# The scores' 32x32 diagonal blocks as a step of their own, ahead of each pair's scores

## The reference, cut to what matters

```python
def step(S, inp):                      # _rwkv7_scan, 8 heads of 64
    r_t, w_t, k_t, v_t, kk_t, a_t = inp
    sa = -jnp.einsum('bhvk,bhk->bhv', S, kk_t)
    S = (S * w_t[:, :, None, :] + sa[..., None] * (kk_t * a_t)[:, :, None, :]
         + v_t[..., None] * k_t[:, :, None, :])
    return S, jnp.einsum('bhvk,bhk->bhv', S, r_t)
...
y = lax.conv_general_dilated(z, conv_w, ...)          # causal, depthwise, width 31
return jax.nn.silu(_layernorm(y + conv_b, ln_g, ln_b, LN_EPS))
...
m = jnp.concatenate([o_c, o_d], axis=-1)              # RWKV group, convolution group
x = x + m @ odd_w_out[j]
```

## Time and profile before

| | us |
|---|---|
| median of 2 runs | 1249.18 (1248.44 to 1249.92) |
| the profiled execution | 1249.62 |
| its span, first to last instruction | 1247.8 |
| TensorE busy in the span | 1208.0 (97%) |
| VectorE busy | 640.9 (51%) |
| ScalarE busy | 399.5 (32%) |
| GpSimd busy | 501.3 (40%) |

### The profile page before, as it was taken

The page is one execution under the profiler, slowest core; times in us unless marked ns, Lnnn a source line. Parts: engine busy times, 40 slices in busy tenths (PEclk is TensorE's granted clock), DMA queues, the critical chain, the costliest instruction groups (busy, mean ns, idle before and its releaser), DMA issues. The chain is left out here.

```text
span 1247.8 us, 19837 instructions
## 1 busy us (share of the span) xinstructions
PE 1208.0 (97%) x7876; PEld 968.2 (78%) x7876; DVE 640.9 (51%) x1032; ACT 399.5 (32%) x578; POOL 501.3 (40%) x368
## 2 busy tenths in 40 slices
PE   7999999999999999999999998989999999999996
PEld 6877778888888888887777766757888888888885
DVE  4524655442114544446789889876545211444333
ACT  5634423222112222226353634343322211222110
POOL 0541435554445555545121220113545444555441
PEclk9999999999999999999999999879999999999998
DMA  7211222222322222231111110102222222222211
GB/s 278 102 68 68 74 96 68 101 101 102 101 101 82 89 98 101 101 101 68 35 69 35 36 68 2 35 2 74 96 102 101 101 101 83 86 101 101 101 67 68
DMA packets 17776, 104.97 MB, mean 84 GB/s; under 512 B 1968, under 2 KB 2480, under 8 KB 6064
## 3 DMA queue, kind: packets, MB, share of 16 engines
q1 hardware_dynamic: 17280, 103.67, 23.9%
q10 hardware_dynamic: 432, 0.38, 0.1%
HBM read 101.94 MB, written 2.10 MB: 83 GB/s over the span
## 5 line engine op out<-in xcount | busy, mean ns | idle before, releaser
L580 POOL TENSOR_TENSOR w_lo<-w_raw,w_hi 128x512 fp32r<-128x512 f32 x360 | 495.6, 1406 | 714.4 <-ACT w_hi L673 266.6
L1013 PE MATMUL ps<-h_hi,w_hi 128*128 128x512 f32 x688 | 275.9, 401 | 0.1
L1013 PE MATMUL ps<-h_lo,w_hi 128*128 128x512 f32 x688 | 268.4, 390 | 0.0
L1013 PE MATMUL ps<-h_hi,w_lo 128*128 128x512 f32 x688 | 268.3, 390 | 0.0
L673 ACT ACTIVATE w_hi<-w_raw 128x2048 fp32r<-128x2048 f32 x50 | 95.7, 1913 | 194.7 <-PE ps L1013 143.4
L1013 PEld LDWEIGHTS ps<-h_hi,w_hi 128*128 128x128 f32 x688 | 129.3, 188 | 35.5 <-issue 8.7
L1013 PEld LDWEIGHTS ps<-h_hi,w_lo 128*128 128x128 f32 x688 | 129.4, 188 | 27.6
L1013 PEld LDWEIGHTS ps<-h_lo,w_hi 128*128 128x128 f32 x688 | 129.5, 188 | 25.7 <-issue 1.0
L1013 PE MATMUL ps<-f_hi,w_hi 128*128 128x512 f32 x384 | 149.4, 389 | 0.0
L1013 PE MATMUL ps<-f_lo,w_hi 128*128 128x512 f32 x384 | 149.4, 389 | 0.0
L1013 PE MATMUL ps<-f_hi,w_lo 128*128 128x512 f32 x384 | 149.4, 389 | 0.0
(11 more groups left out here) (328 smaller groups left out, 1699.8 us busy)
## 6 DMA issues: line engine op xcount, KB each, us to landing
w_raw<-in_weights SPq DMA_DIRECT2D x91, 1024.0 KB, 4.8
x<-in_xT SPq DMA_DIRECT2D x8, 256.0 KB, 6.5
w_raw<-in_weights SPq DMA_DIRECT2D x8, 256.0 KB, 6.9
outT<-x SPq DMA_DIRECT2D x8, 256.0 KB, 2.0
sgu_ln<-in_sgu_ln SPq DMA_DIRECT2D x1, 512.0 KB, 7.4
low_w<-in_low_w SPq DMA_DIRECT2D x1, 512.0 KB, 7.1
masks_f<-in_masks SPq DMA_DIRECT2D x1, 432.5 KB, 5.6
sgu_w<-in_sgu_w SPq DMA_DIRECT2D x1, 256.0 KB, 6.4
```

The costliest lines, as they stand in the source:

```text
L580: piece = pool.tensor_tensor(w_lo[:, j, at], w_raw[:, j, at], w_hi[:, j, at].bitcast(f32), SUB)
L1013: mm = pe.matmul(bank(gb(g) if isinstance(i, int) else g % 2), w, r, start=(k == 0 and m == 0), stop=(k == K - 1 and m == 2))
```

## The change

- `scores(c, 4)` becomes a step of its own, `corner(c)`, on TensorE and VectorE. It comes first of a pair's scores: on TensorE it takes the place that `scores(c, 0)` had, on VectorE it stands just before `scores(c, 0)`.
- Its blocks go to banks 4 and 6 instead of 3 and 4. As the scores use bank 6, `scores(c, 0)` now waits for the four corner copies (`x_step`), and the corner waits for `bonus`.
- `scores(c, 0)` moves back on TensorE: in pair 0 to right before scores 1, in pair 1 to one slice before scores 1, in pair 2 to behind `y(1, 3)`, in pair 3 to behind `y(2, 3)`.
- `tok_tr(c, 0)` waits for U of the pair before, where it waited for its Sp.
- The lists around the convolution's norm change too. On TensorE `conv_mean` 0 stands right behind `scores(3, 3)`, `conv_mean` 1 and 2 come among the transposes `tok_tr(3, ·)`, ahead of the last slices; `conv_mean` 3, `conv_var` and `conv_spread` come ahead of `y(3, 2)`, `g(3, 3)`, `u(3, 3)` and `y(3, 3)`. On VectorE `conv_sub`, `conv_root` and `conv_scale` come ahead of `s(3, 2)`. On ScalarE the squares, the root and all four `conv_silu` come ahead of `cut` 58 part 2, `m(2)` and the copies of `g(3, 3)` and `u(3, 3)`.

The diff, cut: first TensorE's list, then the ends of VectorE's and of ScalarE's list (VectorE's list also gets `corner(c)` before `scores(c, 0)` in each pair), then the code of TensorE's and VectorE's steps.

```diff
-            ("slice", 5, 3), ("slice", 5, 4), ("scores", 0, 0), ("slice", 5, 5), ("slice", 5, 6), ("scores", 0, 1),
-            ("slice", 5, 7), ("slice", 7, 0), ("scores", 0, 2), ("slice", 7, 1), ("slice", 7, 2), ("scores", 0, 3),
-            ("scores", 0, 4), *run("slice", 7, 3, 7), ("zw", 1), ("slice", 7, 7), ("tok_tr", 0, 0),
+            ("slice", 5, 3), ("slice", 5, 4), ("corner", 0), ("slice", 5, 5), ("slice", 5, 6), ("scores", 0, 0),
+            ("scores", 0, 1), ("slice", 5, 7), ("slice", 7, 0), ("scores", 0, 2), ("slice", 7, 1), ("slice", 7, 2),
+            ("scores", 0, 3), *run("slice", 7, 3, 7), ("zw", 1), ("slice", 7, 7), ("tok_tr", 0, 0),
...
-            ("slice", 17, 3), ("g", 0, 2), ("scores", 1, 0), ("u", 0, 2), ("slice", 17, 4), ("slice", 17, 5),
+            ("slice", 17, 3), ("g", 0, 2), ("corner", 1), ("u", 0, 2), ("slice", 17, 4), ("slice", 17, 5),
...
-            ("y", 0, 3), *run("slice", 8, 1, 5), ("scores", 1, 1), ("slice", 8, 5), ("slice", 8, 6),
-            ("scores", 1, 2), ("slice", 8, 7), ("slice", 10, 0), ("slice", 10, 1), ("scores", 1, 3),
-            ("scores", 1, 4), *run("slice", 10, 2, 8), ("zw", 2), ("tok_tr", 1, 0), *run("slice", 9, 0, 8),
+            ("y", 0, 3), *run("slice", 8, 1, 4), ("scores", 1, 0), ("slice", 8, 4), ("scores", 1, 1),
+            ("slice", 8, 5), ("slice", 8, 6), ("scores", 1, 2), ("slice", 8, 7), ("slice", 10, 0), ("slice", 10, 1),
+            ("scores", 1, 3), *run("slice", 10, 2, 8), ("zw", 2), ("tok_tr", 1, 0), *run("slice", 9, 0, 8),
...
-            ("y", 1, 1), ("g", 1, 2), ("u", 1, 2), ("slice", 11, 7), ("scores", 2, 0), ("s", 1, 2), ("y", 1, 2),
-            ("g", 1, 3), ("u", 1, 3), ("y", 1, 3), ("slice", 13, 0), ("slice", 13, 1), ("scores", 2, 1),
-            ("slice", 13, 2), ("slice", 13, 3), ("scores", 2, 2), *run("slice", 13, 4, 7), ("scores", 2, 3),
-            ("scores", 2, 4), ("slice", 13, 7), *run("slice", 12, 0, 3), ("tok_tr", 2, 0), ("tok_tr", 2, 1),
+            ("y", 1, 1), ("g", 1, 2), ("u", 1, 2), ("slice", 11, 7), ("corner", 2), ("s", 1, 2), ("y", 1, 2),
+            ("g", 1, 3), ("u", 1, 3), ("y", 1, 3), ("scores", 2, 0), ("slice", 13, 0), ("slice", 13, 1),
+            ("scores", 2, 1), ("slice", 13, 2), ("slice", 13, 3), ("scores", 2, 2), *run("slice", 13, 4, 7),
+            ("scores", 2, 3), ("slice", 13, 7), *run("slice", 12, 0, 3), ("tok_tr", 2, 0), ("tok_tr", 2, 1),
...
-            ("u", 2, 3), ("scores", 3, 0), ("y", 2, 3), ("slice", 20, 5), ("slice", 20, 6), ("scores", 3, 1),
-            ("slice", 20, 7), ("scores", 3, 2), ("slice", 21, 0), ("slice", 21, 1), ("scores", 3, 3),
-            ("scores", 3, 4), ("slice", 21, 2), ("conv_mean", 0), *run("tok_tr", 3, 0, 3), ("post", 2, 0),
-            *run("slice", 21, 3, 8), ("tx", 3, 3, 0), ("tx", 3, 3, 1), ("post", 2, 1), ("dx", 3, 3, 0),
+            ("u", 2, 3), ("corner", 3), ("y", 2, 3), ("scores", 3, 0), ("slice", 20, 5), ("slice", 20, 6),
+            ("scores", 3, 1), ("slice", 20, 7), ("scores", 3, 2), ("slice", 21, 0), ("slice", 21, 1),
+            ("scores", 3, 3), ("conv_mean", 0), ("slice", 21, 2), ("conv_mean", 1), ("tok_tr", 3, 0),
+            ("conv_mean", 2), ("tok_tr", 3, 1), ("tok_tr", 3, 2), ("post", 2, 0), *run("slice", 21, 3, 8),
...
-            ("conv_mean", 1), ("conv_mean", 2), ("tx", 3, 6, 1), ("dx", 3, 6, 0), ("dx", 3, 6, 1), ("out", 0, 0),
...
-            ("g", 3, 2), ("u", 3, 2), ("out", 0, 1), ("s", 3, 2), ("y", 3, 2), ("conv_mean", 3), ("g", 3, 3),
-            ("u", 3, 3), ("y", 3, 3), *run("conv_var", 0, 4), ("out", 0, 2), ("conv_spread",), ("post", 3, 0),
-            ("post", 3, 1), *run("out", 1, 0, 3), ("post", 3, 2), ("out", 0, 3), ("out", 1, 3), ("out", 0, 4),
...
+            ("u", 3, 1), ("s", 3, 1), ("y", 3, 1), ("g", 3, 2), ("u", 3, 2), ("out", 0, 1), ("s", 3, 2),
+            ("conv_mean", 3), *run("conv_var", 0, 4), ("conv_spread",), ("y", 3, 2), ("g", 3, 3), ("u", 3, 3),
+            ("y", 3, 3), ("out", 0, 2), ("post", 3, 0), ("post", 3, 1), *run("out", 1, 0, 3), ("post", 3, 2),
...
-            *run("tap", 3, 21, 25), ("s", 3, 1), *run("tap", 3, 25, 31), ("s", 3, 2), ("m", 2),
-            *run("conv_sub", 0, 4), ("conv_root",), ("conv_scale", 0), ("post_v", 3, 0), *run("conv_scale", 1, 4),
-            ("post_v", 3, 1), ("m", 3), ("m", 4), ("post_v", 3, 2), ("post_v", 3, 3), *run("m", 5, 8),
+            *run("tap", 3, 21, 25), ("s", 3, 1), *run("tap", 3, 25, 31), *run("conv_sub", 0, 4), ("conv_root",),
+            *run("conv_scale", 0, 4), ("s", 3, 2), ("m", 2), ("post_v", 3, 0), ("post_v", 3, 1), *run("m", 3, 7),
+            ("post_v", 3, 2), ("post_v", 3, 3), ("m", 7),
...
-            ("g", 3, 2), ("u", 3, 2), ("cut", 58, 2), ("m", 2), ("g", 3, 3), ("conv_sq", 0), ("u", 3, 3),
-            *run("conv_sq", 1, 4), ("cut", 58, 3), ("conv_root",), ("ysb", 3), ("post", 3, 0), ("conv_silu", 0),
-            ("conv_silu", 1), ("m", 3), ("m", 4), ("conv_silu", 2), ("conv_silu", 3), *run("m", 5, 8),
+            ("g", 3, 2), ("u", 3, 2), *run("conv_sq", 0, 4), ("conv_root",), *run("conv_silu", 0, 4),
+            ("cut", 58, 2), ("m", 2), ("g", 3, 3), ("u", 3, 3), ("cut", 58, 3), ("ysb", 3), ("post", 3, 0),
+            *run("m", 3, 8),
...
+            def corner(c):
                 pe.wait_ge(*dyn_step("rt", c))
+                pe.wait_ge(s("bonus_done"), c + 1)
+                if c:
+                    pe.wait_ge(s("tx_done"), 2 * MERGES * c)
                     pe.wait_ge(s("x_upd"), 2 * (MERGES - 1) * c)
+                for n in range(TT):
                     for h2, r in enumerate(COLUMN_HALVES):
                         for q in range(0, P, 32):
-                            mm = pe.matmul(ps[q:q + 32, 3 + h2, 32 * n:32 * n + 32],
+                            mm = pe.matmul(ps[q:q + 32, 4 + 2 * h2, 32 * n:32 * n + 32],
                                            bT[r, n * P + q:n * P + q + 32], AR[r, c % 2, n, 0, q:q + 32],
                                            start=True, stop=True)
+                mm.then_inc(s("L_mm"), 1)
+            def scores(c, i):
+                if i:
+                    pe.wait_ge(s("score_done"), 8 * c + 2 * i)
+                else:
+                    pe.wait_ge(s("x_step"), X_STEPS * c + 4)
...
             def tok_tr(c, b):
...
-                        pe.wait_ge(s("Sp_done"), 3 * c)
+                        pe.wait_ge(s("u_done"), 4 * c)
...
-                                        ps[:, 3:5, 0:P].rearrange("p h (t n) -> p t h n", n=32)[:, :, :, BASE * k:BASE * k + BASE])\
+                                        ps[:, 4:7:2, 0:P].rearrange("p h (t n) -> p t h n", n=32)[:, :, :, BASE * k:BASE * k + BASE])\
```

More of the change, by code:

```diff
@@ L444, in build @@
             ("dyn", 0, "bt"), ("dyn", 0, "k2"), ("dyn", 0, "kt"), ("dyn", 0, "rt"), ("dyn", 0, "rk"),
-            ("evac_b", 14), ("evac_a", 15), ("bonus", 0), ("tap", 0, 0), ("tap", 0, 1), ("scores", 0, 0),
-            ("scores", 0, 1), ("evac_a", 5), ("scores", 0, 2), *run("tap", 0, 2, 6), ("scores", 0, 3),
-            ("scores", 0, 4), ("solve", 0, 6), ("evac_b", 5), ("solve", 0, 5), ("solve", 0, 4), ("solve", 0, 3),
+            ("evac_b", 14), ("evac_a", 15), ("bonus", 0), ("tap", 0, 0), ("tap", 0, 1), ("corner", 0),
+            ("scores", 0, 0), ("scores", 0, 1), ("evac_a", 5), ("scores", 0, 2), *run("tap", 0, 2, 6),
+            ("scores", 0, 3), ("solve", 0, 6), ("evac_b", 5), ("solve", 0, 5), ("solve", 0, 4), ("solve", 0, 3),
             ("tap", 0, 6), ("evac_a", 7), *run("tap", 0, 7, 10), ("solve", 0, 2), ("solve", 0, 1), ("scan", 1),
@@ L1325, in bonus @@
                 pe.matmul(bank(6), BLK, rx[:, :], start=True, stop=True).then_inc(s("bonus_mm"), 1)
-            def scores(c, i):
+            def corner(c):
                 pe.wait_ge(*dyn_step("rt", c))
-                if i < 4:
-                    if i:
-                        pe.wait_ge(s("score_done"), 8 * c + 2 * i)
-                    else:
-                        pe.wait_ge(s("bonus_done"), c + 1)
-                        if c:
-                            pe.wait_ge(s("tx_done"), 2 * MERGES * c)
-                            pe.wait_ge(s("x_upd"), 2 * (MERGES - 1) * c)
-                    for lhs, at in ((bT, slice(0, 256)), (kT, slice(256, 512))):
-                        for h2, r in enumerate(COLUMN_HALVES):
-                            ar = AR[r, c % 2, i, :, :].rearrange("p a n -> p (a n)")
-                            mm = pe.matmul(bank(5 + h2, at.start, at.stop), lhs[r, i * P:i * P + P], ar,
-                                           start=True, stop=True)
-                            if lhs is kT:
-                                mm.then_inc(s("score_mm"), 1)
-                if i == 4 and c:
-                    pe.wait_ge(s("g_done"), 4 * c)
-                    pe.wait_ge(s("xt_last"), 2 * c)
@@ L1353, in scores @@
                                            bT[r, n * P + q:n * P + q + 32], AR[r, c % 2, n, 0, q:q + 32],
```

(17 more changed lines are left out.)

20 lines of the change are left out of this document (9 added, 11 removed), and 7 rows, old and new, of the table PE1.

## The result

The changed kernel takes 1276.94 us (median of 2 runs, 1275.96 to 1277.92) for 1249.18: 1.0225 times the kernel before, 95% interval 1.0188 to 1.0263, or +27.8 us. Four more runs of it (e13) give 1277.42 beside 1250.21 (1.0215, 1.0179 to 1.0251). The forecast was 1265, range 1254 to 1273: too low, and the result lies outside the range. Whether the loss is over or under 2% stays open, as both intervals hold 1.02. The profiled execution took 1277.92 with a span of 1276.1.

A forecast was written before the change was run, and what follows sets the result against it. TensorE was taken as busy nearly throughout, with VectorE setting the pace in the last pair's chain. Terms 1.9 + 1.5 + 0.3 + 3.4 + 7.9 + 1.0 = 16.0 on the median 1249.18 gave 1265 us, range 1254 to 1273.

The forecast's parts named there:

- Clock: Tail's holes and the 16 dense slices behind: half-clock stretches there cost +1 us, bounds -3 and +6.
- pair 2: Corner copies start when VectorE is free at 726.14, so the first scores copy comes later: +1.0 less 0.7, +0.3 us.
- pair 0: Scores 0 wait for corner copies behind two slow taps, scores 1 follow directly, zw waits for the last copy: +1.9 us.
- pair 1: Scores 0 one slice ahead of scores 1, VectorE's taps delay later copies: +2.2 less the corner's 0.7, +1.5 us.
- pair 3 and means: Scores lag 1.3 us and conv_means run bare ahead of the last slices, delaying first merge and VectorE's list: +3.4 us.
- chain: Last pair's chain, 798 to 832 us: VectorE's list sets the pace; the sum had no separate term here.
- tail: After the last taps: the convolution's norm ahead of the last chunk loses TensorE's cover, leaving the chain bare: +7.9 us.
- the table load: Tail, ScalarE: second load of 1.28 us before the root; the page's 2.66 would make the tail 1.4 us longer.
- The rival that came true: After the tail's holes TensorE stays at half clock through the dense matmuls: over 1274.2 us; chance 0.07.
- The change doesn't do what it is named for: Rival: the solve starts earlier, the scores' 3.5 us of waits go, 1245 to 1250; not slower at all had 0.05.

The follow-up runs named there:

- e13: The changed kernel again, unedited, in four more runs; 1277.42 us beside 1250.21, ratio 1.0215.
- e8: Kernel before plus 8 dense matmuls nobody reads in TensorE's holes of the last pair's chunk steps; 1246.37 us beside 1248.19, and 1248.35 beside 1249.78 when repeated.
- e9: Changed kernel plus 45 dense matmuls nobody reads: 9 in pair 0's scores, 8 in the last pair's chunk steps, 28 in the tail; 1269.34 us.
- e4: Changed kernel plus 53 dense matmuls nobody reads: 9 in pair 0, 10 ahead of a merge (overwriting a wanted gate product), 34 in the tail; 1270.61 us.
- e10: Kernel before with only the tail's new order, plus 8 dense matmuls nobody reads in the chunk steps and 28 in the tail; 1257.47 us beside 1249.78.
- e1: Changed kernel with the convolution's means and tail in the order of before, so the corner part alone; 1258.52 us beside 1249.35.
- e14: Changed kernel plus 9 dense matmuls nobody reads, in pair 0's scores only; 1273.5 us.
- e5: Kernel before with only conv_mean 0 to 2 moved ahead of the merges as in the changed kernel; 1255.59 us beside 1248.19.
- e2: Kernel before with the changed means and tail, scores and banks as before; 1267.51 us, ratio 1.0144.
- e6: Kernel before with the tail's new order, but ScalarE's four silus again behind the root of y_norm; 1260.56 us beside 1248.19.
- e7: Kernel before with only the tail's new order, plus 13 dense matmuls nobody reads in the tail's holes; 1260.24 us beside 1248.19.
- e3: Kernel before with only the tail's new order, all three engines' lists from the last tap on; 1260.53 us, ratio 1.008.

## Why the prediction was wrong

The step that failed is the term *Clock*: "I take +1, with -3 and +6 as bounds". The rest of the sum, 15.0, comes to 16.8 when it is read at full clock, and 1.4 of that difference is pair 2. The last two columns of the table below are the time that the lower level adds: a landmark stretch minus the same stretch in the kernel of the first table that has it at full clock (e8 for the kernel before; e9, e4 and e10 for the changed order).

| term | predicted | at full clock | half clock, after | half clock, before |
|---|---|---|---|---|
| pair 0 | 1.9 | 18.2 - 16.4 = 1.8 | 3.0 | 0 |
| pair 1 | 1.5 | 69.6 - 68.3 = 1.3 | 0 | 0 |
| pair 2 | 0.3 | 69.4 - 67.8 = 1.7 | 1.9 | 2.2 |
| pair 3 and means | 3.4 | 58.8 - 55.4 = 3.4 | 1.5 | 0 |
| chain | 0 | 0 (taken) | 3.1 | 1.8 |
| tail | 7.9 | 27.8 - 19.2 = 8.6 | 5.3 | 0.9 |
| sum | 15.0 | 16.8 | 14.8 | 4.9 |

16.8 + 14.8 - 4.9 = 26.7, and with 0.6 ahead and 0.9 behind 28.2 of the 28.3 us of span. For the clock that is +9.9 where the forecast had +1 and at most +6. The columns are worked out from single profiles, and the total must come out, as the stretches add up to the span; what the table tells is how it divides. The "0 (taken)" is open: no run had the changed order in the chain at full clock.

- **Pair 0, pair 1, pair 3, the means: right**, to 0.2 us, also where no filler stands: e1 has 18.16 in pair 0, e14 58.78 from the third `zw` to `m_hi`. The corner's copies behind two slow taps, scores 0 and 1 side by side, the bare means ahead of the last slices: each is in the trace.
- **Pair 2: mis-sized**, 1.7 for 0.3. The row that I measured from, a first copy at 726.97 with 0.83 of idle ahead, stood inside a half-clock stretch of its own (725.45 to 728.86). At full clock the copy starts 0.6 earlier behind `bonus(2)` (16.23 in e8 for 16.84), so the base of the sum was late already and the lag looked smaller. In e9 the first copies come 1.6 later than in e8, and behind a tap of 1.59 the lag grows by 0.7 until scores 3, as much as the missing corner gives back. The term's own figures also add up to 728.4, not the 728.1 that it states.
- **The tail: right as a mechanism**, and as a timeline nearly to the tenth. From the taps' end the prediction had the last `out` matmul at 28.0, e10 has 27.8; `G` at 12.1 and 11.9; the root of `y_norm` over at 16.7 and 16.5. The term is 0.7 larger because half clock had made the tail of before 0.9 longer: TensorE came to `conv_mean` 3 0.99 behind the taps' end, in e8 0.06. About the table load, the root starts 0.01 us behind the load's end (863.64 + 1.28, then 864.93), in e10 0.02, where the load in turn starts 0.02 behind the copy ahead of it; the page's figure for load and drain, which the prediction set beside it (the Trainium skill, ScalarE: Activation LUTs, What ACT_TABLE_LOAD costs), is not borne out here.
- **The clock: the mechanism was thought of, and in the wrong place.** I priced the lower level only on the dense slices behind the holes, as 0.2 us more for each matmul. But in a chain in which TensorE waits for others and they for it, each of its short steps is on the path too, with nothing beside it: the mean takes 2.07 for 1.12, the spread 2.04 for 1.13, the transposes 1.97 for 1.09. Of the tail's 5.3 us, 4.3 are there before the first slice that follows: `y_norm`'s transposes end 22.1 behind the taps' end, in e10 17.9. And I looked for falls only where I expected the widest holes. In both profiles of the changed kernel the clock also fell in pair 0, behind holes of 1.3 and 1.5 us; e1, with the same holes, shows that these alone don't bring it.
- **The means in the chain.** I had them costing nothing where they stood, as VectorE sets the pace there. VectorE does set the pace, but they may have done something: in all five profiles with them gone and no filler in the chain, the half-clock stretch there runs through without a break (27.3 us in e5, 34.1 in e2 and the changed kernel, 41.0 in e13 and e14). With them in place the longest is 10.2 before and in e6, 6.8 in e7, 13.7 in e1 and 20.5 in e3, half of that in the tail. No run moved a dense step and nothing else to test it; e5 also has them bare ahead of the merges.
- **The rival that came true** is the one on the other side, over 1274.2, which had 0.07. Its condition, two more long stretches, is met, but not by its mechanism: it put them on the dense slices behind the tail's holes, where only one of 10.2 us came (859.4 to 869.6); the longest lay in the chain, ahead of these holes.
- **The change doesn't do what it is named for:** right. The solve starts no earlier, and the scores' waits rose from 3.5 to 6.3 us.

## What to carry to other kernels

Where TensorE waits inside a chain, price the new idle twice: once as the wait, and once as the chance that what follows runs at half clock, the short steps on the path included; take that price from a row of the same step at either level. Profile the same order more than once before a fall is put down to a hole. Before a row of the old profile becomes the base of a sum, look up whether it lies in a stretch at the lower level. And a dense step that costs nothing where it stands may be what lets the clock come back there; here that is likely, not shown.
